# Products of the modulation vector: from TensorE with the vector as weights to row sums of the transposed matrix on VectorE

## The reference, cut to what matters

```python
x = layer_norm(x, emb_ln_g, emb_ln_b)
cs = jax.nn.silu(c)                                  # (1, 1024)
mod = cs @ w_ada[l] + b_ada[l]                       # (1, 6 * 1024)
sh1, sc1, gt1, sh2, sc2, gt2 = ...                   # six parts of 1024
h = x * (1.0 + sc1) + sh1
p = h @ w_in[l]                                      # gMLP and RWKV inputs
mix = concatenate([y_a, y_b]) @ w_out[l]             # y_a from p: gMLP; y_b: RWKV in chunks
x = layer_norm(ALPHA * x + gt1 * mix, ln1_g, ln1_b)
h = x * (1.0 + sc2) + sh2
gu = h @ w_ffn_in[l]
f = (silu(gu[..., :FFN]) * gu[..., FFN:]) @ w_ffn_out[l]
x = layer_norm(ALPHA * x + gt2 * f, ln2_g, ln2_b)
```

## Time and profile before

| | us |
|---|---|
| median of three executions | 1429.22 |
| lowest and highest | 1426.14, 1432.72 |
| the profiled execution, first to last instruction (span) | 1428.9 |
| TensorE busy | 1371.8 (96%) |
| VectorE, ScalarE, GpSimd busy | 698.6, 566.9, 465.6 |

### The profile page before, as it was taken

The page is one execution under the profiler, slowest core; times in us unless marked ns, Lnnn a source line. Parts: engine busy times, 40 slices in busy tenths (PEclk is TensorE's granted clock), DMA queues, the critical chain, the costliest instruction groups (busy, mean ns, idle before and its releaser), DMA issues.

```text
span 1428.9 us, 23064 instructions
## 1 busy us (share of the span) xinstructions
PE 1371.8 (96%) x9570; PEld 1131.4 (79%) x9570; DVE 698.6 (49%) x1192; ACT 566.9 (40%) x854; POOL 465.6 (33%) x131
## 2 busy tenths in 40 slices
PE   5999999999999999999999999999999999999998
PEld 3788766776788888888888678888798888888886
DVE  6656686464665333353337435687255454453002
ACT  4435654253342223222125445555364433443112
POOL 0243143024314434434522321121212443344344
PEclk9999999998999999999999999999999999999999
DMA  8763266002222232223214420011222223223311
GB/s 333 249 138 118 71 244 220 3 4 84 94 89 89 92 115 89 89 102 134 89 62 164 167 89 31 30 38 53 75 89 89 89 89 114 93 89 109 112 59 59
DMA packets 24741, 147.93 MB, mean 104 GB/s; under 512 B 2716, under 2 KB 3868, under 8 KB 9024
## 3 DMA queue, kind: packets, MB, share of 16 engines
q1 hardware_dynamic: 21128, 134.21, 26.6%
q10 hardware_dynamic: 3512, 12.26, 3.2%
HBM read 141.74 MB, written 4.72 MB: 103 GB/s over the span
## 4 chain that ended last, share of the span: by engine, by line
PE 87%; DVE 7%; ACT 2%; issue 2%; DMA 1%; POOL 1%; SPq 0%; DVEq 0%; ACTq 0%; POOLq 0%
PE bank L2090 24%; PE bank L2092 23%; PE bank L2091 23%; PE bank L2397 5%; PE bank L1168 2%; DMA raw<-in_weights 1%; PE bank L1159 1%; PE bank L1150 1%; DVE xres L1692 1%; PE bank L2276 1%; DVE act_lo L1689 1%; POOL xres L1330 1%; PE bank L2257 1%; DVE bank L1685 1%; PE bank L1077 1%
## 5 line engine op out<-in xcount | busy, mean ns | idle before, releaser
L1301 POOL TENSOR_TENSOR weight_lo<-raw,weight_hi 128x2048 fp32r<-128x2048 f32 (+2 forms) x90 | 415.1, 4612 | 822.9 <-ACT weight_hi L1349 822.8
L2090 PE MATMUL bank<-act_hi,weight_hi 128*128 128x512 f32 (+1 forms) x1136 | 433.1, 381 | 6.0 <-DVE q L879 1.9
L2092 PE MATMUL bank<-act_hi,weight_lo 128*128 128x512 f32 (+1 forms) x1136 | 422.8, 372 | 0.0
L2091 PE MATMUL bank<-act_lo,weight_hi 128*128 128x512 f32 (+1 forms) x1136 | 422.6, 372 | 0.0
L1349 ACT ACTIVATE weight_hi<-raw 128x2048 fp32r<-128x2048 f32 (+1 forms) x98 | 185.2, 1890 | 393.4 <-PE bank L2092 392.3
L2090 PEld LDWEIGHTS bank<-act_hi,weight_hi 128*128 128x128 f32 x1136 | 214.0, 188 | 48.0 <-issue 8.3
L2092 PEld LDWEIGHTS bank<-act_hi,weight_lo 128*128 128x128 f32 x1136 | 213.7, 188 | 38.6
L2091 PEld LDWEIGHTS bank<-act_lo,weight_hi 128*128 128x128 f32 x1136 | 214.1, 188 | 34.7 <-issue 0.5
L2090 PE MATMUL bank<-weight_hi,hid_hi 128*128 128x512 f32 x352 | 136.9, 389 | 0.0
L2091 PE MATMUL bank<-weight_lo,hid_hi 128*128 128x512 f32 x352 | 136.9, 389 | 0.0
L2092 PE MATMUL bank<-weight_hi,hid_lo 128*128 128x512 f32 x352 | 136.9, 389 | 0.0
(11 more groups left out here) (376 smaller groups left out, 1755.3 us busy)
## 6 DMA issues: line engine op xcount, KB each, us to landing
raw<-in_weights SPq DMA_DIRECT2D x120, 1024.0 KB, 4.8
w<-in_w ACTq DMA_DIRECT2D x2, 2048.0 KB, 12.0
bias_rows<-grow ACTq DMA_DIRECT2D x1, 2560.0 KB
xres<-in_x SPq DMA_DIRECT2D x4, 512.0 KB, 5.8
strip<-bias_rows ACTq DMA_DIRECT2D x1, 2048.0 KB, 9.8
out<-xres SPq DMA_DIRECT2D x3, 512.0 KB, 2.6
row_a<-in_ln_g ACTq DMA_DIRECT2D x2, 512.0 KB, 4.1
row_b<-in_ln_b ACTq DMA_DIRECT2D x2, 512.0 KB, 4.9
```

Source lines behind the costliest of these rows:

```text
L1301: pool.tensor_tensor(wlo[i % SPLIT][:, :size], raw[n % RAW][:, :size], whi[i % SPLIT][:, :size], ALU.subtract).then_inc(lo_ready, 1)
L2090: pe.matmul(o, l[0], r[0], start=first, stop=False)
L2091: pe.matmul(o, l[0], r[1], start=False, stop=False)
L2092: return pe.matmul(o, l[1], r[0], start=False, stop=last)
```

## The change

Every unit of the modulation matrix is laid out transposed: partition j holds, for two columns of the matrix, their 1024 numbers in a row. The vector, after its activation, is spread over all partitions by `across`: eight products of a column of it, broadcast, with the identity; ScalarE copies them into `c_row`. VectorE multiplies a row by `c_row` and adds it up in one operation that also takes the bias as its start, so the sum lands as a column.

- ada0 (scale and shift of the first block) in `mod_column`, ahead of `affine_lo` of the same block. `affine_hi` now runs twice: it writes the affine value back into the bank, and then copies the high part from it. `affine_lo` only subtracts.
- ada1 (second scale and shift) in `second_column`: eight units between those of the first projection (`ADA_BEHIND` for the loads, `ADA_BESIDE` for VectorE).
- The gates in four units each, `gate_sums`: the first gate's beside the second chunk group, the second's beside units 4, 7, 10 and 13 of the feed-forward part. Their columns are spread over partitions by `across`: the first gate in two banks in the last chain (before: four), the second after unit 16.
- Pieces of `out1` take the two places in the last chain that the other two gate rows had.
- The identity is loaded ahead of x. The chunk stages share eight banks. `ada_block`, `columns_block`, `ada`, `columns`, `mod_half`, `ada_rows_act` and the bias rows go.

```diff
+ADA_BEHIND = {"r0": 1, "r1": 1, "v0": 2, "v1": 1, "pv0": 2, "pv1": 1}
+ADA_BESIDE = {"k1": 1, "r0": 2, "r1": 1, "v0": 2, "v1": 2}
+GATE_AT, GATE_ROWS_AT = (4, 7, 10, 13), 16
...
-    units = win[:1] + first[:2] + win[1:2] + first[2:] + win[2:] + ada
+    units = win[:1] + first[:2] + win[1:2] + first[2:]
+    for unit in win[2:]:
+        units.append(unit)
+        n = ADA_BEHIND.get(unit[0], 0)
+        units += second[:n]
+        second = second[n:]
+    units += gates[0]
...
+        if m - 1 in GATE_AT:
+            units.append(gates[1][GATE_AT.index(m - 1)])
...
-    b.shared = range(7)
+    b.shared = range(8)
...
-        if n % 2 and n < 8:
+        if n % 2 and n < 4:
             order.append(("mod_rows", n // 2))
...
+        sp.dma_start(ident[:], const("ident")).then_inc(load["ident"], 16)
         for t in range(TT):
             sp.dma_start(xres[:, t, :], src["x"][0, tok(t), :]).then_inc(load[f"x{t}"], 16)
...
+        for j in range(2):
+            await_full(act, ("c_row", j))
+            a.done(act.activation(c_row[:, SEQ * j:SEQ * j + SEQ], bank(("c_row", j))[:], ACT.Copy), drain(("c_row", j), "act"))
...
         def affine_hi(k):
-            await_drained(act, ("cols0", k), "dve")
+            act.wait_ge(S["column_ready"], k + 1)
             await_full(act, ("h1", k))
-            a.done(act.activation(act_hi[:, k, :], bank(("h1", k))[:], ACT.Identity, bias=affine[:, 1, k:k + 1],
-                                  scale=affine[:, 0, k:k + 1]), drain(("h1", k), "act"))
+            full = bank(("h1", k))[:]
+            a.step(act.activation(full, full, ACT.Identity, bias=affine[:, 1, k:k + 1], scale=affine[:, 0, k:k + 1]),
+                   drain(("h1", k), "act"))
+            a.done(act.activation(act_hi[:, k, :], full, ACT.Copy), drain(("h1", k), "act"))
...
+        def ada_sums(name, starts, sums):
+            n = UNIT_AT[name]
+            raw_ready(dve, n)
+            for j, (start, total) in enumerate(zip(starts, sums)):
+                w = raw[n % RAW][:, DM * j:DM * j + DM]
+                d.step(V.tensor_tensor_reduce(out=w, in0=w, in1=c_row, scale=1.0, scalar=start, op0=ALU.mult, op1=ALU.add,
+                                              accum_out=total), ada_used if j else None)
...
+            scale = modc[:, KC + k:KC + k + 1]
+            ada_sums(f"ada0_{k}", (col("b_sh1", k), modc[:, k:k + 1]), (affine[:, 1, k:k + 1], scale))
+            ts(affine[:, 0, k:k + 1], scale, col("emb_g", k))
+            stt(affine[:, 1, k:k + 1], scale, col("emb_b", k), affine[:, 1, k:k + 1], ALU.mult, ALU.add, sem=S["column_ready"])
...
-        low_part("lora0")
-        for k in range(KC):
+        await_drained(dve, ("c_row", 1), "act")
+        mod_column(0)
+        low_part("lora0")
+        affine_lo(0)
+        for k in range(1, KC):
             mod_column(k)
             if k == 1:
                 low_part("k0")
             affine_lo(k)
...
+            for _ in range(ADA_BESIDE.get(name, 0)):
+                second_column(next(seconds))
...
+        def across(name, column, n):
+            for i in range(n):
+                mm = pe.matmul(bank(name)[:, tok(i)], column(i).to_broadcast([P, P]), ident[:], start=True, stop=True)
+            fill(name, mm)
```

More of the change, by code:

```diff
@@ L184, in add @@
         before = {e: self.drains[e][bank] for e in self.drains}
-        if unit is None and ada is None:
+        if unit is None:
             self.fills[bank] += 1
@@ L189, in add @@
         after = {e: self.drains[e][bank] for e in self.drains}
-        by = "filled" if unit is None and ada is None else "unit_used" if ada is None else "ada_used"
-        count = {"filled": self.fills[bank], "unit_used": SPLIT_AT[UNIT_AT[unit]] + 1 if unit else 0, "ada_used": ada}[by]
+        by = "filled" if unit is None else "unit_used"
+        count = self.fills[bank] if unit is None else SPLIT_AT[UNIT_AT[unit]] + 1
         self.of[name] = (bank, count, before, after, by)
@@ L266, in plan_banks @@
         dense(f"up1_{m}", drains=[dict(act=1), dict(dve=1)])
+        if m == GATE_ROWS_AT:
+            for j in range(2):
+                b.add(("gate_rows", j), 4 + j, act=1)
     dense_rows("ff1", f"down1_{FT // 2 - 1}")
@@ L511, in build @@
     work = {n: here(n, [P, SEQ]) for n in ("cs", "kk", "sq")}
-    bias4 = here("bias4", [4, SEQ])
     pair_end = nxt
-    h_temp, _ = place("h_temp", [P, 2, SEQ], F32, pair_at + 12288)
     rps = [operands[q]["ar"][:, 0, :] for q in range(2)]
-    ada_rows = [acc[:, 0:SEQ]] + [operands[q]["ar"][:, 1, :] for q in range(2)]
+    c_row = acc[:, DM:2 * DM]
     squares_y, turned_y = ([operands[q][n] for q in range(2)] for n in ("kt", "bt"))
@@ L1563, in _ @@
         for kind, *args in CHUNK_SCHEDULE:
[L1564 to L1566 removed]
+            if kind == "stage":
                 chunk_act(*args)
@@ L1626, in _ @@
             ffn_first(m)
+            if m == GATE_ROWS_AT:
+                for j in range(2):
+                    await_full(act, ("gate_rows", j))
+                    a.done(act.activation(acc[:, DM + SEQ * j:DM + SEQ * j + SEQ], bank(("gate_rows", j))[:], ACT.Copy),
+                           drain(("gate_rows", j), "act"))
         for n in range(FT // 2 - 2):
@@ new lines, in second_column, with gate_sums @@
+        def second_column(k):
+            scale = modc[:, KC + k:KC + k + 1]
+            ada_sums(f"ada1_{k}", (col("b_sh2", k), modc[:, k:k + 1]), (affine[:, 3, k:k + 1], scale))
+            ts(affine[:, 2, k:k + 1], scale, col("ln1_g", k))
+            stt(affine[:, 3, k:k + 1], scale, col("ln1_b", k), affine[:, 3, k:k + 1], ALU.mult, ALU.add,
+                sem=S["affine1"] if k == KC - 1 else None)
+        def gate_sums(g, n):
+            b = ("b_gt1", "b_gt2")[g]
+            ada_sums(f"ada{2 + g}_{n}", [col(b, 2 * n + j) for j in range(2)], [gate_cols[:, g, 2 * n + j:2 * n + j + 1] for j in range(2)])
+            d.step(V.tensor_copy(stats[:, 0, 0:1], stats[:, 0, 0:1]), S["gate_sums"])
@@ L1749, in _ @@
         d.step(V.memset(grow[:, SEQ:], -NEG), S["future_ready"])
         for n, value in enumerate((LN_EPS, RMS_EPS, 1.0)):
-            d.step(V.memset(eps[:, n:n + 1], value))
-        d.step(V.memset(group_rows, 0.0))
-        for n in range(4):
-            d.step(V.memset(scalars[ROW * n:ROW * n + 1, 0:1], 1.0), S["consts_ready"])
+            d.step(V.memset(eps[:, n:n + 1], value), S["eps_ready"] if n == 2 else None)
         d.step(V.memset(restart[:], 1.0))
```

195 lines of the change are left out of this document (63 added, 132 removed).

## The result

The changed kernel takes 1464.49 us at the median (1462.63 to 1465.63), 2.46% more than the kernel before on the same chip (1427.68; ratio 1.0246, 95% interval 1.022 to 1.0272). The forecast was 1443: the direction was right, the size was not. The profiled execution's span grew from 1428.9 to 1460.8 us, by 31.9.

The account below looks back on a forecast made before the run. TensorE was taken as the bound (87% of the last chain), with gains only where nothing replaces its work. Terms 12 + 11 − 10 − 1 + 2 = +14 on 1428.9 us gave 1443; range 1430 to 1460 (own 1434 to 1456).

Parts of the forecast that it names:

- One row sum: VectorE's sum over 1024 columns, both operands in SBUF: 1.23 us and 0.08 to read it; upper bound 2.4.
- Rival (c): VectorE's row sums run at half rate, 1.1 us more each, giving 1466 us; chance 0.09.
- Head, +12: First modulation's column blocks: loop turns serial, 5.4 us per block against 4.86, and starts later; +12 us, bounds +6 and +15.
- Dense stage, +11: First projection: pu0's load waits for the seventh unit's sums in the ring of three, so its products start late; +11 us.
- load 4.8: Dense stage: pu0's weight load, issued after the seventh unit's sums, lands after 4.8 us.
- smaller waits fall inside this one: Dense stage: smaller waits, such as pv0's through the fourth unit, add nothing beyond the wait at pu0.
- First group, -10: First chunk stages: 17 us of modulation products leave TensorE, 10 of them on the path; -10 us, bounds -17 and -5.
- Last chain, -1: Gate rows before the output projection: fewer products, but TensorE then waits for the low part; -1 us, bounds -10 and +2.
- rest, +2: Second gate's rows cost two times 1.16 us after unit 16; identity load, bias load, extra bank and gate sums cost nothing.
- (a): VectorE's order is loose enough, the ring never late, the dense stage costs nothing: +3, 1432 us; chance 0.11.
- (b): TensorE is the bound everywhere behind the head, so removed products count in full: -13, 1416 us; chance 0.10.
- (d): TensorE gets the slow 1.2 GHz clock, giving back part of the chunk stages' gain: 1449 us; within the forecast's 0.70 chance.

## Why the prediction was wrong, point by point

- **One row sum**, 1.23 and 0.08: measured 1.28 and 0.08. Rival (c), half rate, falls. In the dense stage some sums took 3.4 to 5.5 us while GpSimd's subtraction ran, as I had allowed for squares but not for sums; no run took that apart.
- **Head, +12**: +12.8. The start (17.1) was 16.0, the turn (5.4) 5.37, the bias product (71.6) at 72.16.
- **Dense stage, +11, bounds 0 and 14**: +29.8. The step that failed is "load 4.8": a median over all loads of the kernel, used in a stretch where another transfer runs. The price was in the trace of before, one view further on. Its loads from 60 to 76 us took 20.0 us at the median, those from 76 to 132 took 11.0, and nobody waited:

```profile
raw<-in_weights SPq DMA_DIRECT2D x2, 1024.0 KB, 20.0
...
raw<-in_weights SPq DMA_DIRECT2D x5, 1024.0 KB, 11.0
```

With the write out of the way the term measured 11.4 to 13.0. So the mechanism (pu0 behind the seventh unit's sums, ScalarE's kk, VectorE's square beside GpSimd) was right, and "smaller waits fall inside this one" was right with loads of 5 us and wrong with loads of 21: then r1, v1 and pair 0's squares each waited too. The upper bound of 14 had let the order vary and not the load.
- **First group, -10**: -10.6, but by the wrong account. I had 10 of 17 us of products on the path; the products give 2 to 4 of 10. That the total came out is luck. "One bank more: nothing" may have been wrong by up to 4 us, and some 4 stay open.
- **Last chain, -1, and rest, +2**: 0.0 together. TensorE does stand before the low part, as said; ScalarE's conversions show +1.8 us at the gate rows of unit 16, and 1.6 given back at 816 us. The row of the chain:

```profile
359.62 0.80 PE L2104 MATMUL bank<-weight_hi,act_hi 128*128 128x512 f32 x1 [7.74 <-POOL weight_lo L1304]
```

- **The rivals.** (a), the ring never late, and (b), TensorE the bound behind the head, fall. (d), the slow clock, is seen (a mean of 0.90 in the dense stage) but as a price of the waits, 8.0 of the 29.8 us, and not where I had put it: the chunk group kept 0.98. The result of 1466 for (c) is near the measured one for another reason; the range was set too narrow because the one resource that I didn't give a bound, the transfers, was taken at its median.

## What to carry to other kernels

Before a ring of buffers gets more to carry, list every other transfer in that stretch, and read the time to landing of that stretch, not the page's median: a load that is late today costs nothing and tells what it will cost. An engine's idle share in a chain of two engines is poor cover: there 29 us of added work found 4 us of it. A wait costs more than its own length, since the products behind it run at the slow clock. And when a term comes out right, test its reason as well, with the stretch cut at marks: here the number was right and its reason wasn't.

## What the runs showed of the hardware that was not expected

- A write from eight partitions holds 46.6% of the 16 engines' time for some 50 GB/s, in packets of 2.5 KB, and a 1 MB load issued beside it takes 11 to 24 us in place of 5 (seen in both kernels). That both queues share the engines is what the Trainium skill says (Trainium Kernel Development and Optimization, Key Constraints), and the rows agree. The Trainium skill also says how many engines a transfer gets: the largest number up to 16 that divides its slowest dimensions (DMA: Bandwidth & Descriptors, Why a DMA increments its semaphore by 16 and not by 1). For eight rows that would be eight engines, half of them (an estimate by that page), which 46.6% would fit; no run here shows which engines were busy.
- TensorE stopped 11.4 us for no semaphore, amid small products, while the same write ran beside the chunk group. Whether its instructions came late over the same engines was not tried.
- Four products with 32 columns each cost what one does (1.07 and 1.04 us).
